# Gate projections dealt over nine levels of a recurrence, and 22 unread products ahead of the first norm

## The reference

```python
def _rmsnorm(x, g):
    xf = x.astype(jnp.float32)
    y = xf * lax.rsqrt(jnp.mean(xf * xf, axis=-1, keepdims=True) + NORM_EPS)
    return (y * g.astype(jnp.float32)).astype(x.dtype)

def _hgrn2(h, lb, w_in, out_norm, w_out):
    z = h @ w_in                      # q_pre, f_pre, i_in, g_pre: 1024 columns each
    f = lb + (1.0 - lb) * jax.nn.sigmoid(f_pre)
    log_f, k, q, v = jnp.log(f), 1.0 - f, jax.nn.silu(q_pre), i_in
    ...
    def step(state, inp):             # chunks of the sequence, 8 heads of 128
        b = jnp.cumsum(lfc, axis=2)
        o_inter = jnp.einsum('bhtd,bhde->bhte', qc * jnp.exp(b), state)
        decay = jnp.where(causal, jnp.exp(jnp.where(causal, diff, 0.0)), 0.0)
        a = jnp.einsum('bhtd,bhsd,bhtsd->bhts', qc, kc, decay)
        o_intra = jnp.einsum('bhts,bhse->bhte', a, vc)
        ...
    o = o * lax.rsqrt(jnp.mean(o * o, axis=-1, keepdims=True) + NORM_EPS)
    o = o.reshape(B, S, E) * out_norm * jax.nn.silu(g_pre)
    return o @ w_out
```

## Time and profile before

| | us |
|---|---|
| median of 3 runs (lowest to highest) | 2930.38 (2929.76 to 2933.28) |
| the profiled execution | 2926.07 |
| its span, first to last instruction | 2924.0 |
| TensorE busy (share of the span) | 2892.2 (99%) |
| VectorE busy | 2371.0 (81%) |
| GpSimd busy | 1262.6 (43%) |
| ScalarE busy | 1197.3 (41%) |

### The profile page before, as it was taken

How to read it: one execution, slowest core, us unless ns; L and a number is a source line. 1 busy time by engine, 2 the same in 40 slices (tenths; PEclk the granted TensorE clock), 3 DMA queues, 4 the chain that set the end, 5 groups by cost and what they waited for, 6 DMA issues and landing times.

```text
span 2924.0 us, 43254 instructions
## 1 busy us (share of the span) xinstructions
PE 2892.2 (99%) x15746; PEld 2580.7 (88%) x15746; DVE 2371.0 (81%) x4474; ACT 1197.3 (41%) x1928; POOL 1262.6 (43%) x748
## 2 busy tenths in 40 slices
PE   8999999999999999999999899999999999999998
PEld 7678999999998888888888788999999998888887
DVE  7537999899878888888357758999898978888887
ACT  6543334444433333333437543334444433333333
POOL 4133565334444444442346543664334444444441
PEclk9999999999999999999999999999999999999999
DMA  4132558999999999998321132669999999999995
GB/s 154 34 103 87 167 182 313 367 381 358 372 379 402 356 364 361 360 357 320 106 96 42 44 116 92 201 200 365 363 380 354 378 396 380 362 358 365 357 366 205
DMA packets 346147, 799.97 MB, mean 274 GB/s; under 512 B 27984, under 2 KB 192080, under 8 KB 345680
## 3 DMA queue, kind: packets, MB, share of 16 engines
q1 hardware_dynamic: 235200, 478.32, 47.1%
q0 software_dynamic: 73728, 268.47, 24.1%
q10 hardware_dynamic: 37008, 50.41, 4.7%
HBM read 694.33 MB, written 102.76 MB: 273 GB/s over the span
## 4 chain that ended last, share of the span: by engine, by line
PE 96%; DVE 2%; ACT 1%; issue 0%; POOL 0%; DMA 0%; DVEq 0%; SPq 0%; ACTq 0%
PE PS L1655 29%; PE PS L1657 29%; PE PS L1656 29%; PE PS L1876 3%; PE PS L1855 1%; PE PS L1954 1%; PE PS L1785 1%; PE PS L1786 1%; PE PS L1832 1%; DVE resid L1126 1%; ACT arena L713 0%; PE PS L1820 0%; DVE arena L1531 0%; PE PS L1665 0%; PE PS L1666 0%
## 5 line engine op out<-in xcount | busy, mean ns | idle before, releaser
L700 ACT ACTIVATE w_hi<-w_raw 128x1024 fp32r<-128x1024 f32 x607 | 641.5, 1058 | 766.7 <-PE PS L1657 685.6
L1655 PE MATMUL PS<-x_hi,w_hi 128*128 128x384 f32 (+1 forms) x2564 | 897.3, 350 | 0.0
L1657 PE MATMUL PS<-x_hi,w_lo 128*128 128x384 f32 (+1 forms) x2564 | 886.3, 346 | 0.0
L1656 PE MATMUL PS<-x_lo,w_hi 128*128 128x384 f32 (+1 forms) x2564 | 885.1, 345 | 0.0
L1655 PE MATMUL PS<-w_hi,x_hi 128*128 128x512 f32 x1744 | 679.8, 390 | 3.7 <-POOL w_lo L614 2.9
L1657 PE MATMUL PS<-w_hi,x_lo 128*128 128x512 f32 x1744 | 678.6, 389 | 0.0
L1656 PE MATMUL PS<-w_lo,x_hi 128*128 128x512 f32 x1744 | 678.5, 389 | 0.0
L625 POOL DMA_INDIRECT arena<-in_v_t,arena x256 | 425.4, 1662 | 557.1 <-DVE resid L1418 528.7
L1119 DVE TENSOR_TENSOR w_lo<-w_raw,w_hi 128x1024 fp32r<-128x1024 f32 x448 | 549.4, 1226 | 97.7 <-ACT w_hi L700 85.1
L614 POOL TENSOR_TENSOR w_lo<-w_raw,w_hi 128x1024 fp32r<-128x1024 f32 x159 | 396.1, 2496 | 491.9 <-ACT w_hi L700 491.9
L625 POOL DMA_INDIRECT arena<-in_u_rows,arena x256 | 366.6, 1432 | 508.7 <-DVE arena L1402 454.2
(11 more groups left out here) (207 smaller groups left out, 2302.3 us busy)
## 6 DMA issues: line engine op xcount, KB each, us to landing
w_raw<-in_u_t SPq DMA_DIRECT2D x256, 512.0 KB
w_raw<-in_v_t SPq DMA_DIRECT2D x256, 512.0 KB
acts_dram<-arena ACTq DMA_DIRECT2D x256, 192.0 KB
gates_dram<-arena SPq DMA_DIRECT2D x24, 2048.0 KB
arena<-acts_dram SPq DMA_DIRECT2D x256, 192.0 KB
arena<-gates_dram SPq DMA_DIRECT2D x64, 768.0 KB
w_raw<-in_hg_t SPq DMA_DIRECT2D x40, 512.0 KB
w_raw<-in_pq_t SPq DMA_DIRECT2D x32, 512.0 KB
```

Of the source, the lines that this page charges most:

```text
L700: act.activation(w_hi[:, slot, :], w_raw[:, slot, :], ACT.Copy).then_inc(hi_ready, 1)
L1655: pe.matmul(ps, wh, xh, start=start, stop=False)
L1656: pe.matmul(ps, wh, xl, start=False, stop=False)
L1657: return pe.matmul(ps, wl, xh, start=False, stop=stop)
```

## The change

The gate of head g begins at level 4 + 9(g - 1), takes 2, 1, 2, 1, 1, 1 parts over six levels and none over the next three. Until now it began at level 4 + 8(g - 1), with the same pattern, and the last gate was spread over the last 12 levels one part at a time. ScalarE's tanh and VectorE's silu of a gate move to the level at which the next gate begins, and the high part of a weight tile moves to stand right behind the tanh. The order of the last splits of the gated rows is adapted: two instead of three stand within the last head.

Apart from that, TensorE multiplies a cleared tile with itself 22 times into a PSUM bank that nobody reads, ahead of the first norm, and in the first norm VectorE makes the mean of a tile ahead of the scaling of the tile before it, not behind it.

```diff
-LAST_GATE = [8 * HEADS - k for k in (12, 11, 10, 8, 6, 4, 3, 2)]
-def gate_parts(h, p):
-    n = 8 * h + p
-    if n >= 8 * HEADS - 12:
-        return int(n in LAST_GATE)
-    if n < 4:
+GATE_PARTS = (2, 1, 2, 1, 1, 1)
+def gate_start(g):
+    return 4 + (HEADS + 1) * (g - 1)
+def gate_parts(n):
+    if n < gate_start(1):
         return int(n in (1, 2))
-    return (2, 1, 2, 1, 1, 1, 0, 0)[(n - 4) % 8]
+    return next((GATE_PARTS[n - gate_start(g)] for g in range(1, HEADS)
+                 if 0 <= n - gate_start(g) < len(GATE_PARTS)), 0)
 def gate_finished(n):
-    return n // 8 if n % 8 == 4 and n // 8 < HEADS - 1 else None
+    return next((g for g in range(HEADS - 1) if n == gate_start(g + 1)), None)
...
+            pool.memset(warm, 0.0).then_inc(sem("warm_made"), 1)
             lows(0, BASE["u0"] + FIRST_GATHER)
...
             def gated_high(h):
                 act.wait_ge(sem("gated"), h + 1)
-                if h < 3:
+                if h < HEADS - 1:
                     act.wait_ge(sem("gate_room"), h + 1)
...
-                    if k == 5:
-                        if h < HEADS - 1:
-                            next_high(BASE["hg_g"] + h)
...
                     if gate_finished(8 * h + k) is not None:
                         gate_tanh(gate_finished(8 * h + k))
-                    if (h, k) in ((7, 0), (7, 2), (7, 4)):
-                        gated_high(k // 2)
-
+                        next_high(BASE["hg_g"] + gate_finished(8 * h + k))
+                    if (h, k) in ((7, 4), (7, 5)):
+                        gated_high(k - 4)
+
+            head_scaled(HEADS - 2)
+            gated_high(2)
+            gated_high(3)
             gate_tanh(HEADS - 1)
-            head_scaled(HEADS - 2)
-            gated_high(3)
+            next_high(BASE["hg_g"] + HEADS - 1)
             gated_high(4)
-            next_high(BASE["hg_g"] + HEADS - 1)
...
+                        if k == 0:
+                            mean_square(k, i)
                         if i >= 2 or i == 1 and k not in (2, 4):
                             scale(k, i - 1)
-                        mean_square(k, i)
+                        if k:
+                            mean_square(k, i)
...
             def gated(h):
                 ready(dve, ("turn", h))
+                was_freed(dve, ("hg_g", h))
...
-                if (h, k) in ((7, 1), (7, 3), (7, 5)):
-                    gated_low(k // 2)
+                if (h, k) in ((7, 6), (7, 7)):
+                    gated_low(k - 6)
             mask_level(8 * HEADS - 2)
             mask_level(8 * HEADS - 1)
+            gated_low(2)
+            gated(6)
             gated_low(3)
             gate_silu(7)
-            gated(6)
...
+            pe.wait_ge(sem("warm_made"), 1)
+            for n in range(22):
+                pe.matmul(PS[:, 7, 0:P], warm, warm, start=True, stop=True)
             pe.wait_ge(sem("ident_in"), 16)
             norm(0)
```

More of the change, by code:

```diff
@@ L221, in recurrence @@
                 yield "turn", h - 2, 0
-            for k in range(gate_parts(h, p)):
+            for k in range(gate_parts(n)):
                 yield "gate", part // KC, part % KC
@@ L375, in model @@
         scaled = cut(22176, TT, DM)
+        warm = cut(21504, P)
         act_st = cut(0, RING, D)
@@ L1983, in _ @@
                                x_lo[:, p, :], p == 0, p == KC - 1)
-                    if h == HEADS - 1 and p < 3:
-                        mm.then_inc(sem("gate_room"), 1)
                     if p == KC - 1:
                         end(mm, ("hg_g", h))
+                    elif h == HEADS - 1:
+                        mm.then_inc(sem("gate_room"), 1)
                 elif what == "project":
```

## The result

The changed kernel takes 2936.47 us (median of 18 runs, 2932.48 to 2944.56) where the kernel before, beside it, takes 2930.10 (18 runs, 2927.61 to 2933.28). The ratio is 1.0022, 95% interval 1.0015 to 1.0030: it is 6.4 us slower. The profiled execution took 2936.80 us with a span of 2934.8; TensorE was busy for 2902.6 us of it, 10.4 more than before; the 22 unread products account for 6.5 of these, ahead of the first norm, and no other product was added.

What follows compares the result with a forecast made beforehand. TensorE was taken to be at work almost everywhere, with VectorE also setting the recurrence's pace. Recurrence +4.1 and start -0.95 made +3.2 us, added to 2930.38 for a forecast of 2933.6 us, range 2926.5 to 2938.

Steps and rivals of the forecast that it cites:

- The recurrence, the step that decides: HGRN2 recurrence: gate parts drifting into levels 0 to 3 make VectorE, then TensorE wait; +4.1 us at level 63's product.
- the levels named: Recurrence, heads 3 to 6: VectorE waits for level products at levels 4 to 6, TensorE for mask steps at 6 and 7.
- The lag behind a level product: Recurrence: from the start of a TensorE product to the VectorE step that waits for it, 0.80 us.
- The last head: Recurrence, last head: gains 1.2 us, with two VectorE low parts in place of three and TensorE room for its parts.
- the step that counted nothing for ScalarE: Recurrence: ScalarE's moved tanh and weight-tile high part cost nothing; at most its spare 3.5 us once.
- the moved mean by itself: Start, first norm: the earlier mean lets ScalarE's last root and the chain to the first product come 0.95 us sooner.
- the 22 products count nothing: Start: the unread products run while TensorE waits anyway, so they neither cost nor gain time; counted as nothing.
- Rival (d): Start: TensorE's clock sets the first product; 32 transposes, 149 ns shorter each, give at most -4.8 us, 2928.8; chance 0.03.
- The tail: Behind the recurrence: from level 63's product to the turn 1.23 us, where it was 1.26; later order and waits unchanged.
- (a): Recurrence: the halves even out, each head goes at VectorE's 13.07 us; -4.5 us in all, 2925.9; chance 0.20.
- (b): Recurrence: the halves of a head don't overlap at all, 17.4 us in head 5; +11 us, 2941; chance 0.12.
- (c): Recurrence: no change, the parts fall into free time; only the start's -0.95 us stays, 2929.4; chance 0.10.

Runs made afterwards that it cites:

- e5: Nine-level gates with the old start, plus three or four unread products where TensorE idles at levels 7 and 0: 2935.33 us, 1.0018 against the kernel before.
- e4: Nine-level kernel with the old start, but gates repeat every eight levels and each begins at level 0 of a head: 2935.66 us, 1.0021 against the kernel before.
- e7: Changed kernel with eight-level gates, old last-gate spread, e6's GpSimd order and the second weight tile's high part later: 2924.29 us, 0.9981 against the kernel before.
- e3: Nine-level kernel with the old start, but gates repeat every eight levels, from level 4: 2928.20 us, 0.9999 against the kernel before.
- e1: Changed kernel with the start of before, so only the nine-level gates: 2936.17 against 2928.25 us for the kernel before, ratio 1.0025.
- e8: Kernel before with only the mean moved, without the 22 products; one run: first product at 15.09 us.
- e9: Kernel before with only the 22 unread products, mean not moved; one run: first product at 14.55 us.
- e2: Kernel before with the changed start (22 products and moved mean), old gates: 2927.65 us, ratio 0.9994; first product at 13.90 us.
- e6: Kernel before with GpSimd's low parts of output tiles 2 and 3 ahead of its last head's root: 2925.08 against 2929.53 us, ratio 0.9984.

## Why the prediction was right, and where not

**The recurrence, the step that decides: right in mechanism, too small.** The forecast was +4.1 us at the product of level 63. At the full clock (e5 against before) the eight heads differ by +0.3, +0.3, +0.2, +2.1, +0.4, +1.6, +1.5 and -0.5, in sum +5.9. Head 5 came as reckoned (forecast +1.6) and head 6 within 0.15 of it (+1.4); e4, which holds six parts in levels 0 to 3 all along, gave 14.9 us for the 15.3 worked out. VectorE waits first and TensorE after it, at the levels named or one off. The lag behind a level product was 0.71 to 0.72 us, not 0.80. Four terms were mis-sized.

- Head 3 took 0.9 more than forecast: VectorE's decayed queries (L1587) stand there with 1.58 us where they take 0.68 in most heads, beside a GpSimd subtraction (1601.08 to 1603.32), and one such row of before took 1.08. That GpSimd is the cause was not tried alone; the long steps of e7 stand beside GpSimd's work too.
- Head 4 took 0.5 less than forecast (+0.9).
- Heads 0 and 1 were forecast unchanged and are 0.3 longer each. Head 0 is 0.28 longer also with eight levels (e3), so that is not the drift; head 1 is 0.09 longer there.
- The last head was to be 1.2 shorter, for one low part of VectorE less and for TensorE's room. It is by 0.1 in the changed kernel and by 0.5 in e5. It is by 1.4 in e3, but that is no test of the term: only 2 of the last gate's parts stand in this head there, against 5 before and 7 in the changed kernel. In the changed kernel three of them stand in the first four levels, and TensorE waits 0.83 us for ScalarE at 1657.62, against the step that counted nothing for ScalarE. Which of these takes the gain back was not tried.

**The half clock in the recurrence: missing.** No step asked what the new idle time would do to TensorE itself. The rows give 2.3 us (8.2 less 5.9), by e5 against e1 2.9, and about 1.1 in the output projection (1675.07 to 1679.97 is 4.90 us; before, 1667.26 to 1671.10 is 3.84). The Trainium skill, "TensorE: Matmul & The Clock Gate", Part 1, which the prediction used for the start alone, says that an idle TensorE falls to half its clock. The trace agrees on the two speeds (granted 0.53 and 1.00 in the two stretches of head 5), and shows the fall with TensorE idle for 0.4 to 1.2 us at a time between level products. Which of such places it strikes differs between executions (head 3 in e1, not in the changed kernel).

**The start: a gain, but smaller, and by another step.** The first product came at 14.26 us, between the 13.6 of the forecast and the 14.5 that was named as the sign of being wrong. That the moved mean by itself brings the first product 0.95 us sooner fell with e8, and that the 22 products count nothing fell with e8 and e9. The sign came right by luck: the two moves stood in one kernel, and the one counted as nothing is what lets the other pay. The row of 14.57 named the last of several that came nearly together: with the mean moved, the transposes, the high part of a weight tile that waited 0.24 us for its DMA, and VectorE's low parts stand behind it. The pair of profiles shows -0.31, e2 -0.67 against the profile of before; runs can't tell e2 from nothing. Rival (d) was right that the clock of the transposes can set the first product, and far off in price (-4.8).

**The tail** went as written: 1663.92 to the turn at 1665.18 is 1.26 us, forecast 1.23.

**The rivals.** (a), (b) and (c) are out: none of heads 3 to 6 is at 13.07 us or unchanged, and head 5 is not at 17.4. The forecast of 2933.6 is 2.9 us under the median; its +4.1 and -0.95 stand against +5.9, a clock's 2.3 and 1.1, and -0.3 to -0.7 for the start. These rows sum to 8.6 to 9.0 us, more than the medians' 6.4 and at the upper end of their interval (4.4 to 8.8). The other executions pay less of the clock's part than the profiled one: the mean granted clock is 0.9974 over the 18 runs, against 0.9986 to 0.9988 over the runs of before in the experiments, so by these rounded figures an estimated 3.5 to 4 us of full clock are lost, where the three half-clock stretches of the profile lose 5.1. That the sum lies over the median stays in part open.

## What to carry to other kernels

Where two engines are tied by two buffers, work that fills one engine's gaps must keep its place against the other engine's heavy steps: no gate part was added, and a period of nine levels in place of eight made heads of 13.5 us up to 2.8 us longer, the half clock included. After reckoning a new wait, ask what the idle time does to TensorE's clock behind it. And where a start is ended by several things at once, a row names only the last of them: try each move alone before giving it a price.

## What the runs showed of the hardware that had not been expected

TensorE fell to half clock (granted 0.53 to 0.59 over 3.5 to 4.2 us) in a stage where it was at work between the waits: 3.65 of the 5.50 us ahead of the stretch at 1618.5 are busy. Unread products in those waits kept the clock at 1.00 and made the heads shorter by 0.6 to 1.2 us. In the first 14 us the clock column reads 1.00 while the transposes take 279 ns in one kernel and 384 in another (e9, e6). A transpose of the same shape takes 421 ns in the half-clock stretch of head 6 (1636.15) and 272 behind the one of head 5 (1622.41); in the first norm of e6 the first ones take 417 ns, those at the end 272. So at the start the durations tell the clock, not the column.
